# RWKV chunk inverse on TensorE: 64x64 diagonal blocks in five levels in place of 32x32 blocks in four levels and a corner step

## The reference

```python
def wkv_scan(r, v, decay, k, a_in, b_in, s0, reverse):
    # S_t = S diag(w_t) + (S a_t) b_t^T + v_t k_t^T,  y_t = S_t r_t ;  s0: (B, H, N, N) [value, key]
    def step(S, inp):
        rt, vt, wt, kt, at, bt = inp
        sa = jnp.einsum('bhij,bhj->bhi', S, at)
        S = S * wt[:, :, None, :] + sa[..., None] * bt[:, :, None, :] + vt[..., None] * kt[:, :, None, :]
        return S, jnp.einsum('bhij,bhj->bhi', S, rt)
    xs = tuple(jnp.moveaxis(z, 1, 0) for z in (r, v, decay, k, a_in, b_in))
    s_end, ys = lax.scan(step, s0, xs, reverse=reverse)
    return jnp.moveaxis(ys, 0, 1), s_end
```

## Time and profile before

| | |
|---|---|
| median of 3 runs | 4256.56 us (4256.35 to 4267.2) |
| profiled execution | 4259.65 us, of which the span is 4257.8 us |
| TensorE busy (matmul) | 3909.8 us, 92% of the span |
| VectorE, ScalarE, GpSimd busy | 1027.5, 635.0, 162.0 us |
| instructions | 75390, of them 34690 matmuls and 34690 weight loads |
| the 8 passes of the RWKV mixer | from 2638.5 to 3630 us |

### The profile page before, as it was taken

One profiled execution on the slowest core, in us unless ns is written; L12 is line 12 of the kernel. 1 busy time (PEld: TensorE's weight loads), 2 busy tenths in 40 slices (PEclk: granted clock), 3 DMA queues, 4 the chain that ended last, 5 costly groups with the idle time before them and its releaser, 6 DMA issues.

```text
span 4257.8 us, 75390 instructions
## 1 busy us (share of the span) xinstructions
PE 3909.8 (92%) x34690; PEld 2625.1 (62%) x34690; DVE 1027.5 (24%) x2270; ACT 635.0 (15%) x1453; POOL 162.0 (4%) x262
## 2 busy tenths in 40 slices
PE   5999999999998999689999999888888877999998
PEld 3446645454446667477577685555555556888887
DVE  1000243730113322113003412333333333100001
ACT  2100121510002122011002201111111121000000
POOL 0000000000000000600000000000000000000000
PEclk9999999999999999799999999888888885999999
DMA  8434323233334323975221242101101000444453
GB/s 346 179 122 155 112 87 119 80 129 148 129 128 178 119 101 142 164 226 218 99 79 63 97 146 81 33 33 44 43 24 42 31 25 3 139 148 151 157 167 119
DMA packets 77483, 490.35 MB, mean 115 GB/s; under 512 B 10480, under 2 KB 14576, under 8 KB 23536
## 3 DMA queue, kind: packets, MB, share of 16 engines
q1 hardware_dynamic: 70560, 462.45, 31.0%
q0 software_dynamic: 6608, 23.08, 2.3%
HBM read 481.29 MB, written 4.19 MB: 114 GB/s over the span
## 4 chain that ended last, share of the span: by engine, by line
PE 89%; issue 4%; DVE 4%; DMA 3%; ACT 1%; POOL 0%; DVEq 0%; ACTq 0%; POOLq 0%
PE ps L969 49%; PE ps L1069 9%; PE ps L963 7%; PE ps L908 3%; PE ps L1029 3%; PE ps L1048 2%; PE ps L1230 2%; DMA w<-in_wi 2%; PE ps L966 2%; PE ps L1204 1%; PE ps L1039 1%; PE ps L1092 1%; PE ps L1128 1%; PE ps L1338 1%; PE ps L916 1%
## 5 line engine op out<-in xcount | busy, mean ns | idle before, releaser
L969 PE MATMUL ps<-h,w 128*128 128x256 f32 (+1 forms) x4992 | 1550.8, 462 | 60.4 <-DMA w<-in_wi 43.6
L969 PEld LDWEIGHTS ps<-h,w 128*128 128x128 f32 x4992 | 939.1, 193 | 516.3 <-issue 422.0
L969 PE MATMUL ps<-y,w 128*128 128x256 f32 (+1 forms) x1792 | 507.6, 441 | 0.0
L969 PEld LDWEIGHTS ps<-y,w 128*128 128x128 f32 x1792 | 338.0, 190 | 154.5 <-issue 121.9
L1069 PE MATMUL ps<-h,w 128*128 128x256 f32 (+1 forms) x1024 | 422.2, 537 | 3.1 <-issue 3.0
L963 PE MATMUL ps<-w,h 128*128 128x256 f32 x1280 | 278.6, 379 | 0.0
L963 PEld LDWEIGHTS ps<-w,h 128*128 128x128 f32 x1280 | 243.0, 190 | 38.5 <-issue 6.1
L1069 PEld LDWEIGHTS ps<-h,w 128*128 128x128 f32 x1024 | 187.7, 203 | 103.9 <-issue 80.9
L908 PE MATMUL ps<-w,zone 128*32 128x256 f32 x2304 | 149.8, 402 | 31.5 <-DVE zone L2293 11.7
L1230 PE MATMUL ps<-zone 32*32 32x32 f32 x8192 | 101.3, 203 | 77.4 <-issue 77.4
L1230 PEld LDWEIGHTS ps<-zone 32*32 32x32 f32 x8192 | 89.1, 115 | 100.5 <-issue 100.2
(11 more groups left out here) (315 smaller groups left out, 3225.3 us busy)
## 6 DMA issues: line engine op xcount, KB each, us to landing
w<-in_wm SPq DMA_DIRECT2D x144, 1024.0 KB, 7.9
w<-in_we SPq DMA_DIRECT2D x52, 1024.0 KB, 4.9
w<-in_w SPq DMA_DIRECT2D x48, 1024.0 KB, 4.9
w<-in_wmg SPq DMA_DIRECT2D x48, 1024.0 KB, 4.9
w<-in_wi SPq DMA_DIRECT2D x34, 1024.0 KB, 4.9
w<-in_wo SPq DMA_DIRECT2D x32, 1024.0 KB, 4.9
w<-in_wrw SPq DMA_DIRECT2D x32, 1024.0 KB, 4.9
w<-in_wbr SPq DMA_DIRECT2D x48, 512.0 KB, 4.3
```

Source lines behind the costliest of these rows:

```text
L969: last = mm(pass_psum(s, q), rows[:, n * P:(n + 1) * P], src[k], start=(k == 0), stop=(k == s.kt - 1))
```

## The change

The diagonal blocks are 64x64, a whole chunk, and there are five levels. The corner step, its tiles `o21`, `zs`, `xt64` and its work on TensorE, ScalarE and VectorE are gone; the recurrence multiplies by `xx[:, 0]`. The levels now run token tile by token tile in 20 steps n (level n // 4 + 1, tile n % 4): in each, TensorE issues 8 products of step n (4 for each half of the rows, the halves in turn), some other work (`beside`), 1 or 2 fills, and then the 16 updates of step n - 1 (8 in the last level, which needs x = 0 alone). GpSimd masks a tile at each step, through a ring of 8. `rw_blocks` issues 64 matmuls in place of 128. `rw_keys` moves from ahead of the levels into steps 0 and 1, with banks 7 and 2. The low-rank matmuls and their tanh go by direction in twos. The layout of the zone is shifted accordingly. The diff, cut (shifted addresses, removed semaphores and most removed lines of before are left out, as they stand in the listing above):

```diff
@@ level_masks @@
-    r, c = np.arange(P) % 32, np.arange(32)
+    r, c = np.arange(P) % CH, np.arange(CH)
...
-    parts = [level(l, d) for l in range(1, 5) for d in range(2)]
+    parts = [level(l, d) for l in range(1, 6) for d in range(2)]
...
@@ GpSimd @@
-                for l in range(4):
-                    tt(am[:, l, :, :, :, :].rearrange("p k h d t -> p k h (d t)"),
...
+                for n in range(20):
+                    if n >= 8:
+                        pool.wait_ge(s_pp, 20 * it + n - 7)
+                    tt(am[:, n % 8, :, :, :].rearrange("p h d t -> p h (d t)"),
+                       dsb[:, :, n % 4, :, :].rearrange("p h d t -> p h (d t)"),
+                       lvm[:, n // 4:n // 4 + 1, :, :].rearrange("p o d t -> p o (d t)").broadcast_to([P, 2, 2 * CH]),
+                       ALU.mult).then_inc(s_am, 1)
...
@@ TensorE: rw_rank, rw_blocks, rw_keys @@
+                for a in range(2):
+                    r = half_rows(a)
+                    last = mm(ps[:, 3 - a, :], ranks[r, it % 2, d, :], lowr[r, :], start=True, stop=True)
+                last.then_inc(s_rank, 1)
...
-                            for g in range(4):
+                            for hf in range(2):
                                 for hd in range(2):
...
+                                    at = tok * P + d * 64
+                                    last = mm(ps[half_rows(hf), 3 + 2 * x + hd, at:at + 64], b if x == 0 else a,
+                                              a if x == 0 else b, start=True, stop=True)
+                    last.then_inc(s_mat, 1)
...
-            def rw_keys(it):
+            def rw_keys(it, hd):
...
+                            c = slice(tok * P + 64 * hf, tok * P + 64 * hf + 64)
+                            at = tok * P + d * 64
+                            last = mm(ps[half_rows(hf), 2 if hd else 7, at:at + 64], fbk[half_rows(hd), 1, d, c],
+                                      far[half_rows(hd), d, 0, c], start=True, stop=True)
...
@@ TensorE: rw_invert @@
+                def beside(n):
+                    if n == 0:
+                        pe.wait_ge(s_tre, 5 * it + 1)
+                        rw_keys(it, 0)
+                    elif n == 1:
+                        if it >= 1:
+                            pe.wait_ge(s_yc, 2 * it - 1)
+                        rw_keys(it, 1)
+                    elif n == 2:
+                        pe.wait_ge(s_ake, 2 * it + 1)
+                        rw_transpose(it, 1)
+                    elif n == 3 and it >= 1:
+                        pe.wait_ge(s_ake, 2 * it + 2)
+                        rw_variance(it - 1)
+                    elif n == 4:
+                        pe.wait_ge(s_tre, 5 * it + 2)
+                        rw_transpose(it, 2)
+                    elif n == 5:
+                        pe.wait_ge(s_ake, 2 * it + 2)
+                        if it >= 1:
+                            pe.wait_ge(s_yc, 2 * it)
+                        rw_transpose(it, 3)
+                    elif n == 6:
+                        pe.wait_ge(s_tre, 5 * it + 3)
+                        rw_transpose(it, 4)
+                    elif n == 8:
+                        pe.wait_ge(s_tre, 5 * it + 4)
+                        rw_reads(it, 1)
+                    elif n == 9:
+                        pe.wait_ge(s_tre, 5 * it + 5)
+                        rw_reads(it, 0)
...
-                rw_keys(it)
...
+                for n in range(21):
+                    if n < 20:
+                        tok = n % 4
+                        pe.wait_ge(s_am, 20 * it + n + 1)
+                        if n < 4:
+                            pe.wait_ge(s_x0, 4 * it + n + 1)
                         else:
+                            pe.wait_ge(s_te, 20 * it + n - 3)
+                        if n < 2:
+                            pe.wait_ge(s_dsb, 2 * it + 2)
+                        else:
+                            pe.wait_ge(s_pe, 20 * it + n - 1)
+                        for i in range(4):
+                            for hf in range(2):
+                                r = half_rows(hf)
+                                last = mm(ps[r, 3 + n % 2, i * 64:i * 64 + 64], am[r, n % 8, i // 2, i % 2, :],
+                                          xx[r, 1, tok, i // 2, i % 2, :], start=True, stop=True)
+                        last.then_inc(s_pp, 1)
+                        beside(n)
+                        fill(2 if n % 2 else 1)
+                    if n >= 1:
+                        m, tok = n - 1, (n - 1) % 4
+                        pe.wait_ge(s_pe, 20 * it + m + 1)
+                        if m >= 2:
+                            pe.wait_ge(s_te, 20 * it + m - 1)
+                        for x in range(2) if m < 16 else (0,):
+                                for hf in range(2):
+                                    r, at = half_rows(hf), x * 256 + i * 64
+                                    xt, mine = xx[r, 0, tok, i // 2, i % 2, :], pb[r, m % 2, i, :]
+                                    last = mm(ps[r, 5 + m % 2, at:at + 64], xt if x else mine, mine if x else xt,
+                                              start=True, stop=True)
                         last.then_inc(s_dt, 1)
...
@@ TensorE: end of rw_invert, rw_recur @@
-                pe.wait_ge(s_te, 8 * it + 8)
...
-                last.then_inc(s_z, 1)
...
-                last.then_inc(s_x5, 1)
...
-                pe.wait_ge(s_x6, it + 1)
+                pe.wait_ge(s_te, 20 * it + 20)
...
-                        elif i == 1:
-                            rw_rank(feed, 1)
-                            rw_rank(feed, 2)
-                        elif i == 2:
-                            rw_rank(feed, 3)
+                        elif i < 3:
...
-                            last = mm(ps[r, 5, P + 64 * hd:P + 64 * hd + 64], xt64[r, tok, hd, d, :, :], w1[r, half_rows(hd)],
+                            last = mm(ps[r, 5, P + 64 * hd:P + 64 * hd + 64], xx[r, 0, tok, hd, d, :], w1[r, half_rows(hd)],
...
@@ ScalarE: rw_invert @@
+                for n in range(20):
+                    act.wait_ge(s_pp, 20 * it + n + 1)
+                    if n >= 2:
+                        act.wait_ge(s_dt, 20 * it + n - 1)
+                    f(pb[:, n % 2, :, :].rearrange("p i t -> p (i t)"), ps[:, 3 + n % 2, 0:256], ACT.Copy).then_inc(s_pe, 1)
+                    if n in (2, 4, 5, 6):
+                        transposed({2: 1, 4: 2, 5: 3, 6: 4}[n])
+                    if n == 8 and it >= 1:
+                        rw_root(it - 1)
+                    if n == 12 and it < 7:
+                        rw_raw(it + 1, 2)
...
@@ VectorE: rw_invert @@
+                def update(n):
+                    dve.wait_ge(s_dt, 20 * it + n + 1)
+                    x = slice(0, 2 if n < 16 else 1)
+                    v = xx[:, x, n % 4, :, :, :].rearrange("p x h d t -> p x (h d t)")
+                    v_.tensor_tensor(v, v, ps[:, 5 + n % 2, :].rearrange("p (x t) -> p x t", x=2)[:, x, :], ALU.add)\
+                        .then_inc(s_te, 1)
...
+                for x in (1, 0):
+                    for hd in range(2):
+                        if x == 1:
+                            dve.wait_ge(s_mat, 2 * it + 2)
+                            src = ps[:, 5 + hd, :].rearrange("p (k t) -> p k t", t=2 * CH)
+                        else:
+                            dve.wait_ge(s_dsb, 2 * it + hd + 1)
+                            src = dsb[:, hd, :, :, :].rearrange("p k d t -> p k (d t)")
+                        last = v_.tensor_tensor(xx[:, x, :, hd, :, :].rearrange("p k d t -> p k (d t)"), src,
+                                                lv0[:, x:x + 1, :, :].rearrange("p o d t -> p o (d t)").broadcast_to([P, 4, 2 * CH]),
+                                                ALU.mult)
+                link(last)
+                for tok in range(4):
+                    v = xx[:, :, tok, :, :, :].rearrange("p x h d t -> p x (h d) t")
+                    v_.tensor_tensor(v, v, eye64.rearrange("p (a o t) -> p a o t", a=1, o=1).broadcast_to([P, 2, 4, CH]), ALU.add)\
+                        .then_inc(s_x0, 1)
                 for hd in range(2):
-                    v_.tensor_tensor(mak[:, :, hd, :, :], ps[:, 5 + hd, :].rearrange("p (k d t) -> p k d t", d=2, t=64),
+                    dve.wait_ge(s_ak, 2 * it + hd + 1)
...
+                for n in range(20):
+                    update(n)
+                    if n == 3 and it >= 1:
+                        rw_spread(it - 1)
+                    if n == 7:
+                        reads(1)
+                    if n == 8:
+                        reads(0)
+                    if n == 12 and it >= 1:
+                        rw_readout(it - 1)
+                    if n in (14, 16):
+                        next(mix, None)
```

283 lines of the change are left out of this document (49 added, 234 removed).

## The result

The changed kernel takes 4136.99 us (median of 4 runs, 4124.19 to 4142.74), the kernel before 4256.77 us (median of 4, 4256.35 to 4267.2): a ratio of 0.9711, with a 95% interval of 0.9695 to 0.9726. The forecast was 4183 us and its range began at 4135: the direction was right, the gain was 46 us larger than the sum. The time lies 2 us inside that range, in a part that neither the forecast with its own uncertainties (4146 to 4219 us) nor rival 4 (4154 us) had reached. The profiled execution took 4134.67 us, 125.0 less than the one of before.

The account below looks back on a forecast made before the run. The prediction took instruction supply to bound the invert. Inverts - 48, - 11 and - 10 and recurrences - 5 made - 74 from the profiled 4259.65, so 4186; less 3.1 to the median, 4183 us, range 4135 to 4240.

Parts of the forecast that it names:

- rival 4: Full clock nearly throughout: 63.3 us in passes 1 to 6, 48 in pass 7, recurrence - 9; 4154 us, chance 0.18.
- What bounds the invert: In the inverts, TensorE waits for instruction packets, one each 4.2 us; all 15.4 us of issue gaps in pass 2 go.
- the term for the recurrences: Passes 2 to 5 can win 2.3 us each at the recurrence's start; half was taken, - 5 us in all.
- the row taken as undisturbed: Recurrence of pass 1, 54.1 us at clock 0.96, set against pass 2's 56.4 at 0.92.
- the 0 for the low-rank matmuls: Regrouped low-rank matmuls are as many as before and wanted one chunk later, so they change the time by 0.
- Rival 1: In the inverts, the gaps stay, one for each packet whatever the rate: + 70, 4253 us; chance 0.06.
- Ahead of the levels: Start of an invert: blocks, mean, centring, copies and first identity add take 8.0 us, TensorE waiting some 3.7.
- Steps: Products, updates and fills of the levels: sixteen steps of 2.54 us and four of 2.06, 47.7 us a pass after correction.
- Clock: In inverts of passes 1 to 6, 6 us at the lower clock, 0.43 us lost for each: + 2.6, so 65.9 us.
- Passes 0 and 7: Inverts: pass 0 64.5 us for 75.2, - 11; pass 7, without fills, 56 us, - 10.
- Cover: In the steps, work of VectorE, ScalarE and GpSimd stays hidden; 1 us a step uncovered would cost 20 us a pass.
- Rivals 2 and 3: In the inverts: half the array idle lowers the clock, 4277 us, chance 0.09; diagonal tiles take turns, 4348 us, chance 0.05.

Follow-up runs that it names:

- a6: Changed kernel with each 64x64 product and update issued as two matmuls of 32 weight columns, on four tiles at once: 4217.66 us, ratio 0.9899.
- b3: Kernel before without the updates of the transpose (x = 1), 512 pairs a pass fewer: 4124.07 us, ratio 0.9686.
- a7: Changed kernel with 8 fills in place of 2 ahead of the levels and one in each step: 4092.91 us, ratio 0.9602.
- a11: Changed kernel with the low-rank matmuls and their tanh again in four pieces instead of two: 4143.74 us in one run.
- b4: Kernel before with one fill in place of two behind each product group, so fills last to the corner step: 4237.79 us, ratio 0.9951.
- a1: Changed kernel with each 64x64 product and update issued as two matmuls of 32 moved columns: 4476.63 us, ratio 1.0509.
- a5: Changed kernel with all matmuls of one row half ahead of the other's in each product and update group: 4332.42 us in one run.
- a10: Changed kernel with keys and 8 fills ahead of the levels, shorter VectorE readout and mix pieces, and updates on all four 64x64 tiles: 4049.61 us, ratio 0.95.

## Where the prediction was right, and the step that failed

| us | forecast | measured |
|---|---|---|
| inverts of passes 1 to 6 | - 48 | - 62.8 |
| invert of pass 0 | - 11 | - 14.4 |
| invert of pass 7 | - 10 | - 15.7 |
| recurrences | - 5 | - 30.3 |
| sum | - 74 | - 123.2 |

The measured column is from the two profiled executions, 125.0 us apart; 1.8 us lie outside these stages. What bounds the invert was right. What failed is the term for the recurrences, six times too small, with its two parts: the row taken as undisturbed, and the 0 for the low-rank matmuls. The terms of the inverts were mis-sized by another 24 us together.

**The bound.** Right. Supply held the inverts: the gaps stood 128 matmuls apart or a multiple of it, went with the packets (17 to 9), came back with the instructions (a6), and shrank when 512 matmuls went (b3). Rival 1 is out: 9 packets and no gap. The forecast's count of matmuls, 27010, is the page's.

**Ahead of the levels.** Forecast 8.0 us with 3.7 of waiting; measured 7.4 (2862.80 to 2870.20) with 3.38. GpSimd's mask was priced at 1.08 by the row of before; cut to 256 elements the median is 0.73. VectorE's four copies and the identity add came as priced, within 0.2 each. The add, 1.10 us beside GpSimd's masks, is on the path; the fastest of its kind took 0.68.

**Steps.** Forecast 2.54 us on average, measured (2.60 + 2.18) / 2 = 2.39. The fills are right (0.63 and 1.06). The updates are not: 32 x 30 ns + 0.12 = 1.08 was forecast and 0.98 measured; products 0.56 for 0.60. The change from updates to product, put at 0.12 between 0 and 0.21, is at its lower end, 0.98 - 0.96 = 0.02: here two groups on the same tiles follow each other. 20 x 0.04 + 16 x 0.10 = 2.4 us a pass.

**Clock.** Forecast 2.6 us a pass, for 6 us at 1.2 GHz. The place was right, behind the wait for `xx`; the spell lasted 7 to 10 us and cost 3.6 on average by a7, and about as much by 0.43 for each us. Together 63.3 - 2.4 - 0.6 + 3.6 = 63.9; the mean of passes 1 to 6 is 63.4, for 65.9 forecast: - 62.8 us instead of - 48. Rival 4, full clock throughout, did not come by itself; a7 made it real in passes 0 to 6, with 57.2 instead of its 63.3: the 3.0 of the two corrections above and 2.6 of the wait went too.

**Passes 0 and 7.** Pass 0 took 60.8 us for 64.5; the same steps and copies account for 3.0 of the 3.7. Pass 7 came in 50.1 for 56, at a clock of 0.85: its steps ran at full speed from 18 us into the pass (3441.15). How soon the clock would rise was a guess of the prediction, and a cautious one.

**The recurrences: the step that failed.** Of the 49 us between the two sums, 25 are here. The prediction took pass 1, 54.1 at 0.96, for the undisturbed case, since it was the best row at hand. But a granted clock of 0.96 said that it was not. With the forecast's own 0.43 us lost for each us at the lower clock: 0.04 / 0.5 of 54.1 us are 4.3 us low, 1.9 lost, so 52.2 undisturbed; from pass 2, 56.4 at 0.92, it is 52.5. That is what a11 measured, 52.2 in each pass, and near what b4 comes to (52.3 by the same working, 52.6 in its pass 5). Worked out this way, the rows would have given 55.5 - 52.2 = 3.3 us for each of six passes, 20 us in all, in place of "half of 2.3" for four of them. The rest is the low-rank regrouping, put at 0 for being "as many as before": it is as many, but two now share the array where they used to go alone, 1.2 us a pass. The count of matmuls was the wrong measure; their overlap was the right one. Pass 6, which the term left out, gained 3.5 us, nearly all of it ahead of the first solve too.

**Cover.** Right: in the steps no update waits for VectorE or GpSimd (the waits of pass 2 above). The added masks cost nothing in the steps; whether those that run beside VectorE's first add lengthen it, and with it the wait, no run separates.

**Rivals 2 and 3.** The clock did not suffer from two-tile groups of 64 columns: a7 has the same groups at 1.00 throughout in passes 0 to 6. But a1 fits the rival's mechanism: with 32 columns the inverts fell to 0.80 to 0.87, and pass 7 to 0.51, with no idle time in TensorE's work in the 35 us at 0.50. Rival 3 is out by the 30 ns of the changed kernel, and a5 shows what it would have cost.

**Still open.** Why a1's busy TensorE was granted less. The wait ahead of the levels starts the spell, and it is 3.4 us in both kernels, so it does not explain 35 us in place of 10; what does was not tried by itself, a1 without the wait for instance. The low-rank regrouping was not tried on the kernel before by itself; its 1.2 us a pass come from undoing it alone.

## What to carry to other kernels

Count instructions, not only time in the array: where a group of tiled matmuls runs out of the supply (256 instructions each 3.6 to 4.6 us here), larger tiles that cost the array twice as much can still be faster, and the right tile is the one whose step takes longer than its packets. Fill TensorE's one wait ahead of dense work early: here it was paid twice, 2.6 us a pass as idle time and 3.6 in clock. Where idle time is followed by a low clock, follow the clock past the end of the stage that you change. And when a row is taken as the undisturbed case, look at its granted clock first: if it is under 1.00, work out what the row would be at 1.00.

## What the runs showed of the hardware

- TensorE ran out of instructions only at every 128th matmul or a multiple of that (256 instructions with the weight loads), and packets of 16.4 KB then came 3.6 to 4.6 us apart (before, pass 2).
- A pair on two 64x64 tiles costs 30 ns at full clock with 64 moved columns, and 29.5 with 32 (a1; 55 and 54 ns at the lower clock). On four tiles it is 14 to 16 ns: 64x32 tiles in a6 (64 in 0.92 us) and four 64x64 tiles in a10 (32 in 0.52).
- Diagonal tiles of different row halves write one bank at 30 ns a pair when they alternate and at 54 when they take turns (changed kernel, a5); off-diagonal ones run beside them into another (a10).
- TensorE, busy for 35.00 of 35.00 us, was granted 0.50 of its clock (a1). With the wait at the start cut from 3.38 to 0.80 us it kept 1.00 for whole inverts (a7).
- A matmul of 64 rows and 512 columns takes 1.12 us alone, and 1.13 with its partner of the other row half.
